# The forget gate's logits: one product of stacked split values in place of an FP32 product

## The reference, cut to what matters

```python
z = jnp.einsum('btd,de->bte', h, p['w_in'])
gq, gk, gv, gg, glr, dq, dk, dv = jnp.split(z, _split_points(), axis=-1)
gate_logit = jnp.einsum('btr,rk->btk', glr, p['w_gk2']) + p['b_gk']   # rank 16 -> 256
log_a = (jax.nn.log_sigmoid(gate_logit.astype(jnp.float32)) / GK_NORMALIZER)
S_new, o_g = gla_fn(q_g, k_g, v_g, log_a)
```

## Time and profile before

| What | Value |
|---|---|
| Median of 3 runs | 1342.72 us (1342.07 to 1342.86) |
| Profiled execution, its own time | 1342.28 us |
| Span of its trace, first to last instruction | 1340.1 us |
| PE busy | 1331.6 us, 99% of the span |
| DVE, ACT, POOL busy | 67%, 43%, 30% |
| Mean granted clock of TensorE | 1.000 |

### The profile page before, as it was taken

One profiled execution on the slowest core, in us unless ns is written; L12 is line 12 of the kernel. 1 busy time (PEld: TensorE's weight loads), 2 busy tenths in 40 slices (PEclk: granted clock), 3 DMA queues, 4 the chain that ended last, 5 costly groups with the idle time before them and its releaser, 6 DMA issues.

```text
span 1340.1 us, 23935 instructions
## 1 busy us (share of the span) xinstructions
PE 1331.6 (99%) x8605; PEld 1123.7 (84%) x8605; DVE 896.2 (67%) x1619; ACT 577.6 (43%) x1078; POOL 395.8 (30%) x397
## 2 busy tenths in 40 slices
PE   9999999999999999999999999999999999999999
PEld 8788888777777777887777777677999999999998
DVE  6479667846757776767666674444566665887785
ACT  7464333425645563631424342232454354434532
POOL 3648434455515434341000000000522210332030
PEclk9999999999999999999999999999999999999999
DMA  9458744454365565676658565881665465133301
GB/s 330 125 182 227 238 144 139 141 173 132 98 202 191 179 213 171 215 253 219 236 181 300 181 240 177 294 285 69 213 206 185 162 220 174 48 111 111 111 33 64
DMA packets 126135, 240.33 MB, mean 179 GB/s; under 512 B 13673, under 2 KB 47258, under 8 KB 126018
## 3 DMA queue, kind: packets, MB, share of 16 engines
q1 hardware_dynamic: 116802, 214.68, 48.8%
q10 hardware_dynamic: 9216, 24.14, 5.4%
HBM read 198.16 MB, written 40.62 MB: 178 GB/s over the span
## 4 chain that ended last, share of the span: by engine, by line
PE 96%; DVE 3%; ACT 1%; issue 1%; ACTq 0%; POOL 0%; DVEq 0%; POOLq 0%
PE ps L87 26%; PE ps L89 25%; PE ps L88 25%; PE ps L1576 3%; PE ps L1613 2%; PE ps L1396 2%; PE ps L3424 2%; PE ps L1597 1%; PE ps L428 1%; PE ps L1811 1%; PE ps L490 1%; PE ps L491 1%; PE ps L1437 1%; PE ps L1438 1%; PE ps L452 1%
## 5 line engine op out<-in xcount | busy, mean ns | idle before, releaser
L3182 POOL TENSOR_TENSOR kr<-kr,qb 128x512 f32<-128x512 f32 x128 | 174.3, 1370 | 161.9 <-DVE sd L3167 110.5
L87 PE MATMUL ps<-x2hB,uw_h 128*128 128x264 f32 (+1 forms) x512 | 145.1, 283 | 0.1
L88 PE MATMUL ps<-x2lB,uw_h 128*128 128x264 f32 (+1 forms) x512 | 144.7, 283 | 0.0
L89 PE MATMUL ps<-x2hB,uw_l 128*128 128x264 f32 (+1 forms) x512 | 144.5, 282 | 0.0
L87 PE MATMUL ps<-part_h,fh 128*128 128x264 f32 (+1 forms) x448 | 127.8, 285 | 0.0
L89 PE MATMUL ps<-part_h,fl 128*128 128x264 f32 (+1 forms) x448 | 127.1, 284 | 0.0
L88 PE MATMUL ps<-part_l,fh 128*128 128x264 f32 (+1 forms) x448 | 126.9, 283 | 0.0
L2948 DVE TENSOR_TENSOR xt<-xt,ps 128x264 f32<-128x264 f32 (+1 forms) x224 | 87.4, 422 | 35.8 <-PE ps L89 35.6
L3167 DVE TENSOR_REDUCE sd<-kr 128x8 f32<-128x512 f32 x128 | 85.4, 677 | 35.0 <-POOL kr L3182 35.0
L87 PE MATMUL ps<-uh,dh 128*128 128x512 f32 x256 | 104.1, 406 | 0.9 <-DVE xt L2255 0.8
L87 PE MATMUL ps<-x2hA,uw_h 128*128 128x512 f32 x256 | 104.5, 408 | 0.0
(11 more groups left out here) (395 smaller groups left out, 3406.6 us busy)
## 6 DMA issues: line engine op xcount, KB each, us to landing
kr<-in_cache_k SPq DMA_DIRECT2D x128, 256.0 KB, 3.1
raw_up<-in_w_up_units SPq DMA_DIRECT2D x64, 512.0 KB, 4.1
vr<-in_cache_v SPq DMA_DIRECT2D x128, 256.0 KB, 4.5
raw_dn<-in_w_down SPq DMA_DIRECT2D x32, 512.0 KB, 6.1
raw_dn<-in_w_down ACTq DMA_DIRECT2D x32, 512.0 KB, 4.7
raw<-in_w_in_units SPq DMA_DIRECT2D x23, 512.0 KB, 5.5
raw_up<-in_w_out_units SPq DMA_DIRECT2D x16, 512.0 KB, 4.0
kept_up_low<-uw_l SPq DMA_DIRECT2D x14, 512.0 KB, 6.4
```

Of the source, the lines that this page charges most:

```text
L87: pe.matmul(out, lh, rh, start=first and n == 0, stop=False, skip_group_check=onto)
L88: pe.matmul(out, lh, rl, start=False, stop=False, skip_group_check=onto)
L89: ins = pe.matmul(out, ll, rh, start=False, stop=last and n == len(ks) - 1, skip_group_check=onto)
L3182: pool.tensor_tensor(k[:, :], k[:, :], qb[v // PAGES][:, :], ALU.mult).then_inc(k_multiplied, 1)
```

## The change

The logit product becomes one FP32R product over 96 stacked rows. The 32 low-rank rows are written to rows 96 to 127 of `dg`. From there ACT copies them, rounded to FP32R, into rows 0 to 31 and 64 to 95 of a new tile `low`, and DVE writes the rest (value minus rounded value) to rows 32 to 63. The gate's weights are loaded to rows 96 to 127 of `wgk`; ACT copies them rounded to rows 0 to 31 and 32 to 63 of `wgk_r`, and DVE writes their rest to rows 64 to 95. One product over the 96 rows thus adds high by high, low by high and high by low. `low` and `wgk_r` lie in the memory of `dg` and `wgk`, rows 0 to 95. Two memsets on POOL and a wait of SP for them go.

ACT's part stands at the end of group 11, DVE's part at the start of group 12 behind the splits of units 8 and 9. PE's wait for all three pieces of `low_made` becomes a wait for the piece that it reads, on the semaphore that DVE's new operations raise.

```diff
@@ sync
-                sp.wait_ge(sem("pool_steps"), 8)
...
-                    sp.dma_start(m["wgk"][16 * i:16 * (i + 1), :], a["w_gk2"]).then_inc(gcol_in, 16)
+                    sp.dma_start(m["wgk"][96 + 16 * i:112 + 16 * i, :], a["w_gk2"]).then_inc(gcol_in, 16)
@@ scalar
+            if g == START["low"] + 2:
+                low_highs(act)
@@ gpsimd
-            step.note(pool.memset(low[:, SEQ:NT], 0.0))
-            step.note(pool.memset(m["wgk"][:, :], 0.0))
@@ vector
-            dve.tensor_tensor(low[0:32, c0:c0 + n], ps[0:32, bank_of(g), 0:n], rb[0:32, c0:c0 + n], ALU.mult)\
+            dve.tensor_tensor(dg[96:P, c0:c0 + n], ps[0:32, bank_of(g), 0:n], rb[0:32, c0:c0 + n], ALU.mult)\
...
-            units_first = g in (START["gv"] - 3, START["dk"] + NTILE)
+            units_first = g in (START["low"] + 3, START["gv"] - 3, START["dk"] + NTILE)
...
+            if g == START["low"] + 3:
+                low_lows(dve)
             if units_first:
                 beside(TICK[g])
...
+    def low_highs(act):
+        act.wait_ge(gcol_in, 48)
+        for r in (0, 32):
+            ins = act.activation(wgk_r[r:r + 32, :], m["wgk"][96:P, :], ACT.Copy)
+        ins.then_inc(low_high, 1)
+        for c in range(3):
+            act.wait_ge(low_made, c + 1)
+            if c == 0:
+                act.wait_ge(r_spread, 2)
+            for r in (0, 64):
+                ins = act.activation(low[r:r + 32, columns(c)], dg[96:P, columns(c)], ACT.Copy)
+            ins.then_inc(low_high, 1)
+
+    def low_lows(dve):
+        dve.wait_ge(low_high, 2)
+        dve.tensor_tensor(wgk_r[64:96, :], m["wgk"][96:P, :], wgk_r[0:32, :].bitcast(FP32), ALU.subtract).then_inc(low_low, 1)
+        for c in range(3):
+            dve.wait_ge(low_high, 3 + c)
+            dve.tensor_tensor(low[32:64, columns(c)], dg[96:P, columns(c)], low[0:32, columns(c)].bitcast(FP32), ALU.subtract)\
+                .then_inc(low_low, 1)
@@ gate_tensor
-                pe.wait_ge(low_made, 3)
+                pe.wait_ge(low_low, 3 + c)
                 if i == 0:
                     pe.wait_ge(rb_made, 2)
-                    pe.wait_ge(diag_made, NTILE + 1)
-                    pe.wait_ge(gcol_in, 48)
...
-                pe.matmul(ps[:, logit_bank(i), 0:n], m["wgk"][:, mt * P:(mt + 1) * P], low[:, blk * HALF + off:blk * HALF + off + n],
+                pe.matmul(ps[:, logit_bank(i), 0:n], wgk_r[:, mt * P:(mt + 1) * P], low[:, columns(c)],
```

More of the change, by code:

```diff
@@ L142, in front @@
     dg = at("dg", 170.6875, [P, NT])
-    low = dg
+    low = at("low", 170.6875, [96, NT], FP32R)
+    wgk_r = at("wgk_r", 4.75, [96, 256], FP32R)
     xin = at("xin", 174.75, [P, 3, D_MODEL])
@@ L999, in vector, with columns @@
                 m["late"]["vector"](dve, g - START["gg"] - 3)
+    def columns(c):
+        blk, off, n = PIECES[c]
+        return slice(blk * HALF + off, blk * HALF + off + n)
+    def low_highs(act):
[17 more added lines that the diff above has]
+                .then_inc(low_low, 1)
     def logit_bank(i):
```

## The result

The change made the kernel slower: 1349.54 us (median of 5 runs, 1347.47 to 1350.56) against 1342.25 (5 runs, 1342.07 to 1342.86), a ratio of 1.0047 with a 95% interval of 1.0036 to 1.0059. That is +0.36 to +0.59%, and the median lies above the predicted range, whose upper end was 1347.6. The profiled execution took 1349.72 us, its span 1348.0.

A forecast was written before the change was run, and what follows sets the result against it. PE's list of products was taken as the bound, busy 99% of the span. +5.0 wait - 2.54 saved = +2.5 us; on the profiled 1342.28 that gave 1344.7, plus 0.44 for the median: 1345.2 us, range 1343.9 to 1347.6.

The forecast's parts named there:

- -2.54 us: PE's six logit products: FP32R instead of FP32 saves 1.27 us per block of gate columns, 2.54 us for both.
- 1.91 was predicted: PE's saving on the five logit products after the first: 2.54 - 0.63 = 1.9 us.
- hidden with half a microsecond to spare: ACT's eight copies, 3.78 us, fit into its idle 4.32 us before unit 9's transfer lands at 80.80.
- The wait is 5.0 us: PE waits from 80.2 to 85.2 us, before its first logit product, for DVE's subtractions, with POOL delaying the first.
- the rival that was given 0.05: POOL's second page lands at 84.5 and delays DVE's second subtraction too: about 1.2 us more, +3.7, 1346.4 us; chance 0.05.
- The 3.9 without POOL: PE's wait before the first logit product if POOL does not delay DVE: 3.9 us, +1.4, 1344.1 us; chance 0.12.
- The clock kept: The forecast's own case: PE waits about 5 us before the first logit product and keeps its clock; chance 0.42.
- a rival of 0.33: The clock falls during PE's wait before the first logit product: +4.1 us, 1346.8 us; chance 0.33.
- The rival's price, 1.6: PE's loss if the clock falls in its wait: 13 x 0.125 = 1.6 us, from transposes at the span's start.
- I put nothing more there: DVE's lateness up to group 22: PE and DVE both come about 2.5 us late, so no further cost.
- The 2 us that DVE was to regain: DVE regains about 2 us after POOL's first four pages, by a faster operation and first scan.

The follow-up runs named there:

- E1: The changed kernel with DVE's four subtractions moved ahead of the splits of units 8 and 9 in its list: 1341.66 us, ratio 0.9991 to the kernel before.
- E3: The changed kernel, with POOL's first product with a page of keys waiting for the last of DVE's four subtractions: 1346.88 us, ratio 1.0026 to the kernel before.
- E6: The kernel before, FP32 products kept, with only a wait added: PE's first logit product waits for unit 9's low split; 1346.98 us, ratio 1.0032.
- E2: The changed kernel with 44 unused 128x128 transposes on PE ahead of its wait for the first piece: 1347.70 us, ratio 1.0031 to the kernel before.
- E7: E1 with DVE's own results of groups 19 to 21 ahead of its side jobs: 1342.43 us, ratio 0.9998 to the kernel before.
- E10: E1 with DVE's own results of groups 19 to 23 first and unit 11's split right behind unit 10's: 1346.05 us, ratio 1.0029 to the kernel before.
- E13: E10 with the first recurrence's steps (job "recurA") one tick later on all engines: 1349.85 us, ratio 1.0045 to the kernel before.
- E5: The changed kernel with DVE's subtractions between the low splits of units 8 and 9: 1345.35 us, ratio 1.0018 to the kernel before.
- E12: The kernel before with only DVE's own results of groups 19 to 23 first and unit 11's split right behind unit 10's: 1344.61 us, ratio 1.0018.
- E4: E1 with the logit products put back to FP32, in two passes over the same 96 rows: 1342.55 us, ratio 0.9995 to the kernel before.

## Why the prediction was wrong

- **"-2.54 us", the products: right.** In the chain after, the second logit product takes 0.13 us where it took 0.43. E1, undisturbed, shows 2.47 us for all six. In the kernel after the lateness falls by 1.87 over the other five (8.61 to 6.74), where 1.91 was predicted.
- **The copies on ACT, "hidden with half a microsecond to spare": right.** 3.85 us against 3.78, with 0.24 left.
- **"The wait is 5.0 us": the mechanism right, the size off.** It was 6.0 by PE's row, and PE was held 6.14 at the place. POOL was counted once, but got in at both subtractions: the rival that was given 0.05. That rival's condition, a page landing by 84.5, was put too narrowly: POOL's second product needs only to start before DVE's second subtraction (84.93 against 84.95). The 3.9 without POOL was exact (E3).
- **The clock kept: wrong; this choice failed.** The forecast rested on it, against a rival of 0.33. The granted clock fell to 0.50 inside the wait and stood there until about 92 us. The lateness grew from 6.59 at the first logit product to 8.61 at the second, and the first one's saving of 0.63 was spent in it as well: 8.61 - 6.59 + 0.63 = 2.65 us. The rival's price, 1.6, came from the start of the span; there the granted clock reads 1.00, so those rows do not show the clock's fall that they were taken to price. The rivals were priced one at a time, and here two came true together. That it was the wait, and not the new operations, is shown by E6; that PE kept busy avoids it, by E2.
- **"I put nothing more there", the late DVE: wrong, small.** The 2 us that DVE was to regain came: the operation that took 1.75 us took 0.68, the scans behind it 1.37 instead of 2.34. But from the result of group 15 to that of group 19 DVE, working without a gap, took 22.96 us (104.45 to 127.41) where it had taken 22.24 (97.70 to 119.94). The lateness rose again from 6.74 to 7.45 at group 22 and 7.93 at the first recurrence step, 1.19 us, with the waits at those two places that the result shows.
- **The sum.** 0.45 ahead of the wait, + 6.14 from 80.65 to 86.79 at the place, + 2.65 clock, - 0.63 - 1.87 saved, + 1.19 late DVE = 7.93, against 7.9 in the spans. The 0.45 is not the change's: at the same place E2, whose program is the changed kernel's up to there, is 0.04 early (79.93), and E6, whose program is that of before up to there, is 0.78 late (80.75).
- **What stays open.** E1 ends 1.2 us under the kernel before by the medians, at the edge of what these runs tell. That all of the 2.5 us can be had by some order is not shown: E7, E10 and E13 each moved the wait to a later DVE result, which in E10 waited for a transfer itself.

## What to carry to other kernels

A saving on the bounding engine is worth only what its partners can follow: before counting it, look along the next hundred microseconds for the places where that engine already waits a few tenths, or where a result comes just in time. Put new work for a partner engine by when its inputs are ready, not beside work of the same kind: four small subtractions (2.0 us unhindered) made the kernel 0.56% slower behind a split that waits for a transfer than ahead of it. When a change opens a wait of some microseconds on TensorE in front of a stretch that is bound by it, count the clock's fall as likely and price it by the products that follow at half pace.

## What was not expected of the hardware

- The clock fell after waits much shorter than the 6.0 us: 3.9 (E3), 2.6 (E5 and E6) and, in E12, 1.2. Length alone does not tell: in E1 PE waited 1.6 us at about 120 us and the granted clock stayed at 1.00. In E12 the recurrence's short products stand between the wait and the fall; the same products in E1, without the wait, left the clock at 1.00.
- It also fell without a wait. In the profiled executions of E4 and E10 it was 0.50 for some three microseconds, from about 621 us in E4 and 623 in E10, behind 32 products over 8 rows that took 1.96 us; in the kernel before the same products left it at 1.00. PE lost about 1.5 us there, so one execution says little about a gain of that size. A window of E4:

```profile
622.00:623.00 1.00, 1.00 (x4) 0.80 (x3) 1.00 (x4) 0.00 (x0) 1.00 (x1) 0.50 0.96 385
```

- Two engines' queued operations took turns: DVE's two subtractions, free 0.42 us and some 0.7 for the first piece, took 1.37 and some 1.8 beside POOL, each ending with or just after one of POOL's products, and POOL's next one started between them.
